# Router by replacement, one-pass biases and a reordered front in a routed-expert transformer block

## The chip, the cores and the metric

The kernel runs on one core of a Trainium2 chip. The metric is the device time of one execution in microseconds, and the median of three runs stands for the kernel. In this text PE is the matrix engine (TensorE), DVE the vector engine, ACT the scalar engine, POOL the GpSimd engine and SP the engine whose queue issues most of the DMAs. An arrow, as in ps<-ring, is output from input.

## The reference

The input is 256 tokens of 1024 numbers, all in float32, one layer. What is computed, cut to the parts that matter here:

```python
h = rmsnorm(x, mix_norm_g);  proj = h @ w_in
gates = sigmoid(proj[..., o_g:] + b_branch_gate)
y_pool = multiscale_pool(u_pool, pool_w, pool_scale) @ pool_up
o = rmsnorm(diff_attention(q, k, v, lam), subln_g) * (1 - lam_init)
y_attn = o @ attn_up
x = x + (g_pool * y_pool + g_attn * y_attn) @ w_out
h2 = rmsnorm(x, ffn_norm_g)
logits = h2 @ router_w + router_b                     # 256 x 32
top_v, top_i = top_k(logits, 4);  top_p = softmax(top_v)
comb = sum(one_hot(top_i, 32) * top_p[..., None], axis=1)
for e in range(32):                                   # three 1024 x 1024 weights each
    g = minimum(h2 @ w_gate[e] + b_gate[e], 7)
    u = clip(h2 @ w_up[e] + b_up[e], -7, 7)
    act = (u + 1) * (g * sigmoid(1.702 * g))
    x = x + comb[:, e] * (act @ w_down[e] + b_down[e])
```

## The kernel before, in words

Every large weight comes in pieces of 2 MB, each 128 rows of 4096 numbers, into a ring of eight slots. SP issues the pieces in the order in which they are used, and before each it waits until the piece that last held the slot has been used. There are 12 pieces of the front (w_in in 8, pool_up, attn_up, and w_out in two column halves, `WO_P` and `WO_P + 1`) and then 192 pieces of the experts, six for each of 32 experts: two of w_gate, two of w_up, two of w_down.

**The front.** Its products are exact enough for float32 by splitting both operands into a high part (ACT, `hi_part`) and a low part (DVE, `lo_part`), each piece in four quarters, and by three one-pass products in the type fp32r (`mm3`). Their results pass through two banks of PSUM in turn ("strips"): the product of strip n has to wait until the reader of strip n-2 has released its bank (`strip_start`, `strip_release`). After the attention, PE computes eight strips of y_pool (`up("pup", ...)`); DVE reads each one, multiplies it with its gate and releases the bank (the loop over `("pup", m)`). Then come four gate strips, the transposes of the attention's heads, four more gate strips, eight strips of y_attn (`up("aup", ...)`) and the four projections `project(t, half)`, token tile t by column half of w_out. DVE adds each projection to the residual stream (`residual`), ACT squares it (`squares2`), PE transposes it (`turn_stream`).

**The router.** PE makes the logits with eight small products in four column groups, ACT copies them out, PE transposes them, DVE adds the four groups. DVE finds the top 8 values (MAX8), their places (FIND_INDEX8), compares them with a row of numbers, and sums the comparisons to `chosen`, a 128 x 32 mask for each token tile. Three products with a triangular matrix and a matrix of ones turn the mask into each token's rank in its expert's list. From the ranks `select` makes the first expert's selection matrix `pick`, PE gathers the expert's tokens (`gather(0)`), ACT copies them, PE transposes them (`turn`), DVE multiplies with the norm's gain into `h_in`, and the loop over the experts begins. Meanwhile DVE counts the rounds (the largest list in blocks of 64 tokens; the engines read the number into a register) and builds the weights `comb_tab`.

**The loop.** For each expert PE runs six `product`s of one piece, 64 tokens wide in column halves that run side by side on two halves of the array, in plain float32. Ahead of each of the three pairs stand the `biases`: two matmuls with a selector `this_e` of the expert's row and `bias_rows`. Between the pairs stand `scatter` of the expert before (after the first pair), and after the second pair `gather` of the next expert and three groups of transposes. DVE, ACT and POOL work beside this.

The loop of SP is the one that ties the experts to the memory:

```python
sp.wait_ge(piece_done, at * (UNROLL * PIECES_PER_EXPERT) + (n - SLOTS + 1))
...
sp.dma_start(ring[:, ORDER[n % SLOTS], :], src).then_inc(slot_in[ORDER[n % SLOTS]], 16)
```

The first eight expert pieces wait for the front's pieces in their slots instead (`LEFT_BY`, `front_piece_free`): the last two of them for the fourth projection, the two before them for the third.

## Time and profile before

| What | Value |
|---|---|
| median of 3 runs | 1121.17 us (1120.26 to 1121.29) |
| profiled execution | 1120.66 us, span 1118.9 us |
| PE busy | 1087.1 us (97%) |
| DVE busy, ACT busy, POOL busy | 280.6, 187.2, 30.3 us |
| DMA | 432.55 MB, queue q1 busy 92.1% of 16 engines' span |
| mean granted clock of PE | 0.993 of full |

The span runs from the first to the last instruction. A granted clock of 1.00 is PE's upper level, 2.4 GHz, and 0.50 the lower, 1.2 GHz. The front lasts to about 194 us, the loop over the experts from there to about 1112 us, and the rest is the last expert's way out.

### The profile page before, as it was taken

Reading aid. Unit: us, or ns where it says so; the run is one execution under the profiler, and the core shown is the slowest. Engines: PE = TensorE matmul, PEld = TensorE weight load, DVE = VectorE, ACT = ScalarE, POOL = GpSimd, SP = SyncE. Lnnn points to the kernel's source line nnn. Section 1 sums busy time; section 2 is a strip of 40 time slices with the busy share of each in tenths; the row PEclk is TensorE's granted clock in tenths of the full one; section 3 lists DMA queues with packets and bytes.
Section 4 is the critical chain, followed back from the end, with each engine's and each line's share of the span. In section 5 each row is a group of like instructions: output and inputs, shape, how many; then the busy total and the mean of one; then the engine's idle time right before and its main releaser. Section 6 shows DMA issues by size and latency. Waiting matters only on the chain.

```text
span 1118.9 us, 13222 instructions
## 1 busy us (share of the span) xinstructions
PE 1087.1 (97%) x5385; PEld 464.6 (42%) x5385; DVE 280.6 (25%) x627; ACT 187.2 (17%) x339; POOL 30.3 (3%) x42
## 2 busy tenths in 40 slices
PE   7998997999999999999999999999999999999998
PEld 3887994333333333333333333333333333333332
DVE  4875655111111111111111111111111111111112
ACT  4656432000010001000100010001000100010000
POOL 0070030000000000000000000000000000000000
PEclk9999998999999999999999999999999999999999
DMA  9724487899999999999999999999999999999995
GB/s 320 275 89 176 151 314 302 342 421 426 428 429 427 428 431 427 428 429 430 426 429 429 429 426 429 430 426 429 429 429 427 429 430 426 429 429 430 427 428 223
DMA packets 43486, 432.55 MB, mean 387 GB/s; under 512 B 5829, under 2 KB 6378, under 8 KB 18890
## 3 DMA queue, kind: packets, MB, share of 16 engines
q1 hardware_dynamic: 42906, 431.60, 92.1%
q10 hardware_dynamic: 560, 0.68, 0.2%
q8 instruction: 13, 0.21, 0.1%
q14 instruction: 7, 0.06, 0.0%
HBM read 431.22 MB, written 1.05 MB: 386 GB/s over the span
## 4 chain that ended last, share of the span: by engine, by line
PE 85%; DVE 10%; ACT 2%; SPq 1%; issue 1%; DMA 1%; DVEq 0%; ACTq 0%
PE ps L751 59%; PE ps L758 8%; PE ps L723 6%; PE ps L716 3%; DVE arena L1327 3%; PE ps L489 2%; PE ps L491 2%; PE ps L490 2%; DVE ring_r L1058 2%; DVE arena L1325 2%; ACT ring_r L812 1%; DMA ring<-in_w_in 1%; SPq L433 1%; PE ps L776 1%; PE ps L710 0%
## 5 line engine op out<-in xcount | busy, mean ns | idle before, releaser
L751 PE MATMUL ps<-ring,arena 128*64 128x512 f32 x3072 | 675.6, 592 | 0.0
L751 PEld LDWEIGHTS ps<-ring,arena 128*64 128x64 f32 x3072 | 221.1, 137 | 438.1 <-issue 438.1
L1315 DVE TENSOR_SCALAR arena<-ps 128x512 f32<-128x512 f32 x32 | 22.1, 692 | 473.2 <-PE ps L751 473.2
L758 PE MATMUL ps<-arena 128*64 128x512 f32 x384 | 102.1, 610 | 1.4 <-issue 0.7
L1325 DVE TENSOR_SCALAR arena<-ps 128x512 f32<-128x512 f32 x32 | 22.1, 692 | 235.5 <-PE ps L751 235.5
L967 ACT COPY arena<-ps 128x512 f32<-128x512 f32 x32 | 18.8, 586 | 325.0 <-PE ps L710 325.0
L723 PE MATMUL ps<-arena 64*128 64x512 f32 x264 | 65.6, 615 | 0.8 <-ACT arena L973 0.8
L710 PE MATMUL ps<-arena 128*64 128x512 f32 x264 | 64.1, 607 | 0.8 <-DVE arena L1260 0.8
L965 ACT ACTIVATE arena<-arena 128x512 f32<-128x512 f32 x32 | 20.1, 629 | 242.8 <-DVE arena L1315 242.8
L973 ACT COPY arena<-ps 128x512 f32<-128x512 f32 x32 | 18.7, 585 | 248.7 <-PE ps L751 248.7
L489 PE MATMUL ps<-ring_r 128*128 128x256 f32 (+1 forms) x192 | 59.7, 311 | 0.6 <-DVE arena_r L1141 0.3
L490 PE MATMUL ps<-ring_r 128*128 128x256 f32 (+1 forms) x192 | 57.7, 301 | 0.0
L491 PE MATMUL ps<-ring_r 128*128 128x256 f32 (+1 forms) x192 | 57.7, 301 | 0.0
L1058 DVE TENSOR_TENSOR ring_r<-ring,ring_r 128x1024 fp32r<-128x1024 f32 x44 | 54.0, 1281 | 7.4 <-ACT ring_r L812 7.2
L716 PE MATMUL ps<-con,arena 128*128 128x128 f32 x260 | 40.8, 280 | 6.2 <-DVE arena L1327 5.4
L812 ACT CAST ring_r<-ring 128x1024 fp32r<-128x1024 f32 x44 | 43.7, 1052 | 18.8 <-PE ps L491 10.8
L716 PEld LDWEIGHTS ps<-con,arena 128*128 128x128 f32 x260 | 28.9, 141 | 36.1 <-DVE arena L1327 33.6
L758 PEld LDWEIGHTS ps<-arena 128*64 128x64 f32 x384 | 21.8, 135 | 51.1 <-issue 42.9
L723 PEld LDWEIGHTS ps<-arena 64*128 64x128 f32 x264 | 22.8, 186 | 43.1 <-issue 43.1
L489 PEld LDWEIGHTS ps<-ring_r 128*128 128x128 f32 x192 | 36.6, 190 | 3.5 <-ACT arena L837 0.6
L490 PEld LDWEIGHTS ps<-ring_r 128*128 128x128 f32 x192 | 36.6, 191 | 1.4 <-issue 0.2
L491 PEld LDWEIGHTS ps<-ring_r 128*128 128x128 f32 x192 | 36.6, 191 | 1.3
(183 smaller groups left out, 590.7 us busy)
## 6 DMA issues: line engine op xcount, KB each, us to landing
ring<-in_exp_w_gate SPq DMA_DIRECT2D x64, 2048.0 KB, 19.6
ring<-in_exp_w_up SPq DMA_DIRECT2D x64, 2048.0 KB, 21.8
ring<-in_exp_w_down SPq DMA_DIRECT2D x64, 2048.0 KB, 21.8
ring<-in_w_in SPq DMA_DIRECT2D x8, 2048.0 KB, 8.7
ring<-in_w_out SPq DMA_DIRECT2D x2, 2048.0 KB, 7.6
xt<-in_x SPq DMA_DIRECT2D x4, 512.0 KB, 6.8
ring<-in_pool_up SPq DMA_DIRECT2D x1, 2048.0 KB, 7.4
ring<-in_attn_up SPq DMA_DIRECT2D x1, 2048.0 KB, 7.3
```

The costliest lines, as they stand in the source:

```text
L489: mm(dst, a[0], b[1], start=start, stop=False)
L490: mm(dst, a[1], b[0], start=False, stop=False)
L491: return mm(dst, a[0], b[0], start=False, stop=stop)
L710: last = mm(ps[BLOCK * half:BLOCK * (half + 1), 6, :], pick[:, buf, t, :], h2[:, t, HALF * half:HALF * (half + 1)], start=(t == 0), stop=( ...
L716: last = tr(ps[:, bank, P * c:P * (c + 1)], src[:, P * c:P * (c + 1)], ident)
L723: last = mm(ps[:, 2 * t + half, :], pickT[rows, P * t:P * (t + 1)], y_e[rows, :], start=False, stop=True, skip_group_check=True)
L751: last = mm(ps[BLOCK * half:BLOCK * (half + 1), bank, :], src[:, c, k % 2, :], slot(n)[:, c, HALF * half:HALF * (half + 1)], start=False, ...
L758: mm(ps[BLOCK * half:BLOCK * (half + 1), bank, :], this_e[:, buf, k, :], bias_rows[:, HALF * half:HALF * (half + 1)], start=True, stop=False)
L812: nc.scalar.copy(quarter(hi, q), quarter(ring[:, n % LAND, :], q)).then_inc(w_hi, 1)
L1058: return v.tensor_tensor(dst, whole_ap, hi.bitcast(F32), ALU.subtract)
L1325: v.tensor_scalar(u1, ps[:, 5, :], LIMIT, -LIMIT, ALU.min, ALU.max).then_inc(expert_step, 1)
L1327: v.scalar_tensor_tensor(out=act_out.rearrange("q (c p) -> q p c", c=4), in0=u1.rearrange("q (p c) -> q p c", c=4), scalar=1.0, in1=gs.rea ...
```

## The change

Six things change together.

1. Beside pool_up's strips, DVE no longer makes three low quarters of the gate piece `GB_P` ahead of the first release. It makes quarter 1 before the sums over the heads, quarter 2 after strip 1 and quarter 3 after strip 2; `head_norms` moves from strip 1 to strip 4. ACT squares the last heads (`head_squares(1)`) ahead of its last two high quarters.
2. The four projections run by halves of w_out: (0,0), (1,0), (0,1), (1,1), with a half's transposes after the next projection. The first half of w_out is thus free after two projections.
3. The logits are made by 16 products with the tokens on the output's partitions (`token_logits`), 8 of them ahead of the last transposes. The copy, the transposes and the sum of four groups go.
4. The chosen experts are found by MATCH_REPLACE: the four largest logits are replaced by a number `NEVER`, and where the result differs from the logits the expert is chosen. The mask, the triangle and the ones are bf16 (`chosen`, `counts`). The softmax is taken over all 32 logits with the mask as factor. The second tile's norm (`normed(1)`) moves behind the mask.
5. A bias is one matmul in fp32r instead of two in float32. `bias_rows` holds the high parts of both column halves and their remainders in four groups of 32 rows, for which SP loads the biases with 12 DMAs of 64 KB ahead of the second half of w_out, ACT copies 128 x 1536, and DVE subtracts 128 x 1536. In the loop `name_expert` is one copy of 128 x 128 instead of three of 128 x 64.
6. POOL gets a fill of `four` and a cast of the triangle and the ones; ACT's three bias DMAs and POOL's fill of the unused bias rows go.

```diff
@@ sync
+                if n == PUP_P + LAND:
+                    for k, name in enumerate(("exp_b_gate", "exp_b_up", "exp_b_down")):
+                        for row in range(4):
+                            half = row // 2
+                            sp.dma_start(bias_raw[E * row:E * (row + 1), k, :],
+                                         A[name][0][:, HALF * half:HALF * (half + 1)]).then_inc(bias_in, 16)
...
@@ tensor
+            def token_logits(t, q):
+                for c in range(4 * q, 4 * q + 4):
+                    last = mm(ps[:, 4 + t, 0:E], x2T[:, c, P * t:P * (t + 1)], rw[:, c, :],
+                              start=(c == 0), stop=(c == NC - 1))
+                return last
...
                         def biases(k, bank):
-                            for half in range(2):
-                                mm(ps[BLOCK * half:BLOCK * (half + 1), bank, :], this_e[:, buf, k, :],
-                                   bias_rows[:, HALF * half:HALF * (half + 1)], start=True, stop=False)
+                            mm(ps[:, bank, :], this_e[:, buf].rearrange("p h s -> p (h s)"), bias_rows[:, k, :],
+                               start=True, stop=False, skip_group_check=True)
...
@@ scalar
+                if step == STEPS_ATT - 1:
+                    head_squares(1)
                 for n, q in ahead[step]:
                     hi_part(n, q)
-            head_squares(1)
...
@@ vector
+            lo_part(GB_P, 1)
             own(head_sums(1))
...
-            for q in range(1, PARTS):
-                lo_part(GB_P, q)
...
-                if m == 1:
+                if m in (1, 2):
+                    lo_part(GB_P, m + 1)
+                if m == 4:
                     head_norms()
...
+            own(v.tensor_copy(four[:, :, 0:TOPK], top[:, :, 0:TOPK]))
+            for t in range(NT):
+                last = v.match_replace(left[:, t, :], four[:, t, :], logit[:, t, :], NEVER)
             own(last)
-            v.tensor_reduce(chosen, eq4.rearrange("p t k e -> p t e k"), AX.X, ALU.add).then_inc(chosen_ready, 1)
...
+            v.tensor_tensor(chosen[:], left, logit, ALU.not_equal).then_inc(chosen_ready, 1)
+            v.tensor_scalar(negtop, top[:, :, 0], -1.0, None, ALU.mult).then_inc(top_ready, 1)
+            normed(1)
```

Where the instructions stand now is seen best row by row. First DVE beside pool_up, from the sums over the second tile's heads to the fourth release. L1058 before (L1078 now) is a low quarter, L1164 (L1182) the release of a pool_up strip, L1113 (L1133) the sums, L1147 (L1168) the next small step. Before:

```order
L1113 TENSOR_REDUCE small<-arena 128x4
L1147 SCALAR_TENSOR_TENSOR small<-small 128x8
L1058 TENSOR_TENSOR ring_r<-ring,ring_r 128x1024 x3
L1164 SCALAR_TENSOR_TENSOR arena<-arena,ps 128x256 x2
L1153 RECIPROCAL small<-small 128x8
```

And of the change:

```order
L1078 TENSOR_TENSOR ring_r<-ring,ring_r 128x1024
L1133 TENSOR_REDUCE small<-arena 128x4
L1168 SCALAR_TENSOR_TENSOR small<-small 128x8
L1182 SCALAR_TENSOR_TENSOR arena<-arena,ps 128x256 x2
L1078 TENSOR_TENSOR ring_r<-ring,ring_r 128x1024
L1182 SCALAR_TENSOR_TENSOR arena<-arena,ps 128x256
```

One low quarter now stands ahead of the sums, none between the sums and the first two releases, and one after the second release.

Second, PE after the last projection, to the first gather. L668 (L687) are transposes of the residual stream, L685 (L693) the logits, L690 the transposes of the logits, L695 (L716) zero fills of PSUM, L698 to L702 (L721 to L725) the ranks and counts. Before:

```order
L668 MATMUL ps<-con,xt 128x128 x8
L685 MATMUL ps<-arena 32x256 x8
L690 MATMUL ps<-con,arena 128x128 x2
L695 MATMUL ps<-zrow 128x512 x4
L698 MATMUL ps<-arena,con 128x32
L699 MATMUL ps<-arena,con 128x32
L700 MATMUL ps<-arena,con 128x32
```

And of the change:

```order
L687 MATMUL ps<-con,xt 128x128 x4
L693 MATMUL ps<-arena 128x32 x8
L687 MATMUL ps<-con,xt 128x128 x4
L693 MATMUL ps<-arena 128x32 x8
L716 MATMUL ps<-zrow 128x512 x4
L721 MATMUL ps<-chosen,counts 128x32
L722 MATMUL ps<-chosen,counts 128x32
```

Half of the logits' products moved ahead of the last transposes, and the transposes of the logits are gone.

Third, DVE from the logits to the ranks. L1204 (L1237) is the norm of a token tile, L1228 (L1256) the finished logits, L1232 (L1260) the top 8, L1251 (L1272) the ranks. Before:

```order
L1204 TENSOR_SCALAR arena<-xt,small 128x128x4 x2
L1226 TENSOR_REDUCE arena<-ps 128x64
L1228 SCALAR_TENSOR_TENSOR arena<-arena,small 128x32 x2
L1232 MAX top<-arena 128x8 x2
L1234 TENSOR_TENSOR topw<-top 128x8
L1237 MAX_INDEX topi<-top,arena 128x8 x2
L1239 CAST topf<-topi 128x16
L1241 TENSOR_TENSOR arena<-con,topf 128x128 x2
L1244 TENSOR_REDUCE arena<-arena 128x64
```

And of the change:

```order
L1256 SCALAR_TENSOR_TENSOR arena<-ps,small,arena 128x32 x2
L1260 MAX top<-arena 128x8 x2
L1263 COPY four<-top 128x2x4
L1265 MATCH_REPLACE arena<-four,arena 128x32 x2
L1267 TENSOR_TENSOR chosen<-arena 128x64
L1268 TENSOR_SCALAR small<-top 128x2
L1237 TENSOR_SCALAR arena<-xt,small 128x128x4 x2
L1272 TENSOR_TENSOR arena<-ps,chosen 128x64
```

The way from the finished logits to the mask has four steps after MAX instead of five wider ones, and the norm of the second tile stands behind the mask and ahead of the ranks.

## Rows read from the trace of the kernel before

**Rows 1.** Busy time by stage, the loop: length; busy of PE, PEld, DVE, ACT, POOL; clock; DMA share; GB/s.

```profile
300.00:1100.00 800.00, 794.82 (x3740) 276.46 (x3740) 134.79 (x334) 82.89 (x146) 0.00 (x0) 1.00 1.01 428
```

**Rows 2.** DMA issues from 300 to 400 us, and from 1060 to 1080 us: KB each, us to landing.

```profile
ring<-in_exp_w_gate SPq DMA_DIRECT2D x8, 2048.0 KB, 13.4
...
ring<-in_exp_w_down SPq DMA_DIRECT2D x2, 2048.0 KB, 32.4
```

**Rows 3.** Timeline of SP's queue: start, length over all issues of the row, operation.

```profile
118.72 12.23 SPq L436 DMA_DIRECT2D ring<-in_w_out  x2
142.96 0.82 SPq L456 DMA_DIRECT2D ring<-in_exp_w_gate  x2
...
198.19 3.76 SPq L456 DMA_DIRECT2D ring<-in_exp_w_up  x2
...
1068.49 3.76 SPq L456 DMA_DIRECT2D ring<-in_exp_w_down  x2
```

**Rows 4.** Timeline of PE over one expert: start, length, operation; L758 biases, L751 products, L710 gather.

```profile
502.34 7.04 PE L751 MATMUL ps<-ring,arena 128*64 128x512 f32 x32
...
510.07 7.04 PE L751 MATMUL ps<-ring,arena 128*64 128x512 f32 x32
...
519.86 7.04 PE L751 MATMUL ps<-ring,arena 128*64 128x512 f32 x32
...
526.73 1.89 PE L710 MATMUL ps<-arena 128*64 128x512 f32 x8
...
531.03 1.46 PE L751 MATMUL ps<-ring,arena 128*64 128x512 f32 x6
```

**Rows 5.** Timeline of PE, first projection: start, length, operation, of one of three products.

```profile
154.07 0.40 PE L489 MATMUL ps<-ring_r,arena_r 128*128 128x512 f32 x1
...
154.77 0.39 PE L489 MATMUL ps<-ring_r,arena_r 128*128 128x512 f32 x1
```

**Rows 6.** The chain that ended last, its end: start, length, work.

```profile
1104.86 6.89 PE ps L751 x32
```

**Rows 7.** Timeline beside pool_up, and ACT's w_out parts: start, length, operation, [idle before].

```profile
99.79 0.47 ACT L862 ACTIVATE arena<-ps,small 128x256 f32<-128x256 f32 x1 [2.06 <-PE ps L491]
...
102.04 0.60 ACT L886 ACTIVATE arena<-ps 128x512 f32<-128x512 f32 x1
...
102.67 0.69 DVE L1113 TENSOR_REDUCE small<-arena 128x4 f32<-128x512 f32 x1 [5.25 <-ACT arena L886]
...
103.48 3.49 DVE L1058 TENSOR_TENSOR ring_r<-ring,ring_r 128x1024 fp32r<-128x1024 f32 x3
...
107.35 0.58 PE L489 MATMUL ps<-arena_r,ring_r 128*128 128x256 f32 x1 [4.33 <-DVE arena L1164]
...
143.34 3.88 ACT L812 CAST ring_r<-ring 128x1024 fp32r<-128x1024 f32 x4
```

**Rows 8.** Busy time by stage, single microseconds, columns as in the first group.

```profile
112.00:113.00 1.00, 1.00 (x6) 1.00 (x6) 0.13 (x1) 0.00 (x0) 0.00 (x0) 0.50 0.00 0
113.00:114.00 1.00, 1.00 (x10) 1.00 (x9) 0.29 (x1) 0.00 (x0) 0.00 (x0) 0.92 0.00 0
...
190.00:191.00 1.00, 1.00 (x4) 0.00 (x0) 0.93 (x4) 0.00 (x0) 0.00 (x0) 0.50 0.99 426
```

**Rows 9.** The chain that ended last, the router: start, length, work.

```profile
177.54 0.70 DVE xt L1194
...
181.04 1.30 DVE arena L1204 x2
182.59 0.43 DVE arena L1228 x2
...
185.92 0.43 PE ps L699 x2
...
187.84 3.70 PE ps L710 x8
...
194.73 6.87 PE ps L751 x32
```

More of the change, by code:

```diff
@@ L27 @@
 I32 = mybir.dt.int32
-U32 = mybir.dt.uint32
 P = 128
@@ L48 @@
 MASKED = -1e30
+NEVER = 3e38
 HALF = 512
@@ L175, in build @@
         pickw = part(2 * NT * 2 * BLOCK).rearrange("p (b t h s) -> p b t h s", b=2, t=NT, h=2)
-        this_e = part(2 * 3 * BLOCK).rearrange("p (b k s) -> p b k s", b=2, k=3)
-        bias_rows = part(D)
+        of_expert = part(2 * E).rearrange("p (h e) -> p h e", h=2)
+        assert taken[0] <= places["p"]
+        taken[0] = places["p"]
+        places["bias"] = taken[0]
+        part(3 * HALF)
+        bias_rows = arena_r[:, places["bias"]:places["bias"] + 3 * HALF].rearrange("p (k n) -> p k n", k=3)
+        places["bias_raw"] = taken[0]
+        bias_raw = arena[:, taken[0]:taken[0] + 3 * HALF].rearrange("p (k n) -> p k n", k=3)
+        places["expert"] = taken[0]
+        part(2 * P)
+        this_e = arena_r[:, places["expert"]:places["expert"] + 2 * P].rearrange("p (b h s) -> p b h s", b=2, h=2)
         rank_tab = part(NT * (ROUNDS + 1) * E).rearrange("p (t n) -> p t n", t=NT)
@@ L350, in build, with wo_count @@
         FRONT = len(front)
+        WO_ORDER = [(0, 0), (1, 0), (0, 1), (1, 1)]
+        def wo_count(t, half):
+            return WO_ORDER.index((t, half)) + 1
         LAND, HIS, H_SLOT = 4, 3, 7
@@ L680, in _ @@
+            pe.wait_ge(zero_row, 1)
             pe.wait_ge(rw_ready, 1)
-            pe.wait_ge(x2T_even, NT)
-            pe.wait_ge(x2T_odd, NT)
-            for k in range(2):
-                for c in range(4):
-                    last = mm(ps[E * c:E * (c + 1), 4, 0:S], rw[:, 4 * k + c, :], x2T[:, 4 * k + c, :],
-                              start=(k == 0), stop=(k == 1))
-            last.then_inc(logit_done, 1)
-            pe.wait_ge(logitT_ready, 1)
-            for t in range(NT):
-                last = tr(ps[:, 6 + t, 0:P], logitT[:, P * t:P * (t + 1)], ident)
@@ L924, in _ @@
                 nc.scalar.copy(m_split[0][:, m, :], gate[:, NC + m, :]).then_inc(m_hi, 1)
+            act.wait_ge(bias_in, 16 * 12)
+            nc.scalar.copy(bias_rows, bias_raw).then_inc(bias_hi, 1)
             def squares2(t, half):
-                act.wait_ge(x2_ready, 2 * t + half + 1)
-                fn(junk2[half], xt[:, t, HALF * half:HALF * (half + 1)], ACT.Square,
+                act.wait_ge(x2_ready, wo_count(t, half))
+                if half:
+                    act.wait_ge(x2_sq, wo_count(t, 0))
+                fn(junk2[t], xt[:, t, HALF * half:HALF * (half + 1)], ACT.Square,
                    accum_out=ss2[:, t, half:half + 1]).then_inc(x2_sq, 1)
@@ L1286, in _ @@
                                    op0=ALU.is_gt, op1=ALU.add).then_inc(rounds_ready, 1)
-            for t in range(NT):
-                last = v.tensor_tensor(eq4w[:, t], eq4[:, t], wide(topw[:, t, :], [P, TOPK, E], 2), ALU.mult)
-            own(last)
-            own(v.tensor_reduce(combf, eq4w.rearrange("p t k e -> p t e k"), AX.X, ALU.add))
+            dve.wait_ge(top_exp, NT)
+            own(v.tensor_tensor(expo, expo, chosen[:], ALU.mult))
+            own(v.tensor_reduce(esum, expo, AX.X, ALU.add))
+            own(v.reciprocal(esum, esum))
+            own(v.tensor_tensor(combf, expo, wide(esum, [P, NT, E], 2), ALU.mult))
             own(v.tensor_copy(comb_tab.rearrange("p t (r e) -> p t r e", e=E),
```

156 lines of the change are left out of this document (76 added, 80 removed).

## The prediction

> **What bounds the kernel now.** I read the busy time by stage first. In the loop PE is busy 794.82 of 800 us, and the DMA engines are full as well, at 428 GB/s [rows 1]. Both can't be the bound, so I asked which gains on the other. The view of the DMA issues answers it: a 2 MB piece lands 13.4 us after its issue early in the loop and 32.4 us after it at the end [rows 2]. A slot is asked for as soon as PE has left it, so a growing time to landing means that PE frees slots faster than the memory fills them. PE needs 531.03 - 502.34 = 28.69 us for an expert [rows 4]. The memory needs, for six pieces of 2.097 MB (12.58 MB) at 428 GB/s, about 29.4 us, 4.9 us a piece. The reader is to see in this that the kernel before is bound by PE, but runs down a reserve of landed pieces by 0.7 us an expert, and that the reserve is nearly used up. The last pair of pieces is issued from 1068.49 on, about 1.9 us apart [rows 3]; with 32.4 us [rows 2] the last piece lands near 1070.4 + 32.4 = 1102.8, call it 1103.1. The last two products run from 1104.86 for 6.89 us [rows 6], so the second starts at 1108.3. The reserve left is 5 us. Whatever PE saves in the loop beyond that is not to be had; the end is then set by when the stream of pieces starts, and the stream's bound start is the end of the first product, 194.73 + 3.44 [rows 9], where SP issues again, at 198.19 [rows 3]. From there to the last landing are 1103.1 - 198.2 = 904.9 us for 184 pieces (184 x 4.9 = 901, the rest first latency and short gaps).
>
> So two numbers matter: how much earlier the first product of the loop ends, and what follows the last landing.
>
> **Part by part: the loop.** A pair of biases is worth the difference of the product pairs' starts less the pair itself: 510.07 - 502.34 = 7.73, less 6.87, is 0.86 us [rows 4]. The new one is a single fp32r product, 512 columns wide. Its nearest row is the projection's: three such products in 154.77 - 154.07 = 0.70 us, 0.233 each [rows 5]. Its bounds are that and 0.43, the step of the float32 products (6.87 us for 16 pairs); I take 0.23, since type and shape agree. PE saves 3 x 0.63 = 1.9 us an expert, and its period falls to 26.8 us, 2.6 under the memory's. Over 32 experts that is 60 us of PE's time. The reserve (the ninth piece, issued when the first product ends, lands some 6 us later and is wanted 26.8 + 9.2 - 3.4 = 32.6 us later) is 26 us and gone after ten experts, and from there PE waits for landings. `name_expert` as one copy lies under PE's products and costs nothing.
>
> In that state the pieces land 4.9 us apart. After the second piece's product PE needs the scatter and a bias, today 519.86 - 516.94 = 2.9, then 2.3 us, so the third piece starts 0.8 us after its landing; the fourth starts at its landing. Then come gather, transposes and a bias, today 531.03 - 526.73 = 4.3 us [rows 4], then 3.7, so the fifth starts 3.44 + 3.7 - 4.9 = 2.2 after its landing and ends 0.8 after the sixth has landed. The end is the last landing + 0.8 + 3.44 (product) + what follows the last product today, 1118.9 - 1111.75 = 7.15 [rows 6]: 11.4 us.
>
> **The front, pool_up.** PE stood idle for 4.33 us until DVE gave the first strip back [rows 7]. The rows say why: DVE waited 5.25 us for ACT's squares at 102.04, which stood behind two high parts, and then made three low quarters, 3.49 us, ahead of the first release. And the granted clock was at 0.50 until 113.1 [rows 8], after that idle time: two strips took 113.08 - 107.35 = 5.7 us where at 1.00 a strip of 12 products of 256 columns takes half as long, 2.8 for both. In the new order the squares come right after the last gate's tanh (99.79 + 0.47 [rows 7]), at about 100.3 to 100.9; the low quarter 1 is done in the wait for them. The sums end at 101.6 (0.69), the small step at 101.8, and the first release at 102.2, before PE is through with the second strip (102.8 = 107.35 - 4.33, less a little). The second release comes at 103.4; a low quarter (1.17 us, a third of 3.49) and a release (0.42) make 1.6 us twice, against 1.4 us a strip on PE, with one strip of slack. So PE doesn't wait, the low quarters are done before the gate strips ask for them, and `head_norms` (about 1.6 us, after strip 4) fits as well. Sum: 4.5 + 2.9 = 7.4 us. What is late next is PE itself: from there to the router it has no wait worth a number, and ACT, DVE and the loads of w_out and of the first expert are released by PE, so all of it shifts. SP's 12 bias loads stand ahead of the second half of w_out. Its queue waits there anyway, 12.23 us for two issues [rows 3]; an issue costs 0.41 (two in 0.82) to 1.9 us (two in 3.76) [rows 3], so 12 cost 5 to 23 us. I take 5, the small end, because the dear ones are issues into a full queue. At the other end w_out's second half is issued 11 us late. Today it is issued at 130.9 and ACT comes to it at 143.34 [rows 7], 12.4 us later; a piece with a free queue needs about 8, so ACT, behind which the copies for the first projection queue, would be late by 6 us. ACT's copy and DVE's subtraction of 128 x 1536 are 1.6 us each by the rate of the low quarters (1.17 for 1024), and they lie under the first projection: without that cover they cost 1.6 us once. POOL's two operations lie under the q and k products.
>
> **The front, router.** I count from P, the end of the last projection, 177.54 [rows 9], to the first product of the loop at 194.73: 17.2 us. Now: 4 transposes 0.45; 8 small float32 products of 128 x 32, 0.215 each, 1.7; 4 transposes 0.45; 8 more, 1.7, with DVE's copy of the last half hidden under the first four. Price: 0.43 for one at clock 0.50 [rows 9], halved for 1.00, since PE is busy throughout. Logits at P + 4.5; today at 182.59, P + 5.05. From there DVE needs 0.43 (logits), 0.3 (MAX), 0.2 (copy), 0.4 (two replacements, bounded by nothing and by the 0.43 of rows of the same shape; taken near it), 0.2 (compare): mask at P + 6.1. Then DVE makes the first scale, 0.2, and the second tile's norm, 1.3 in the row of 181.04, of which the next step waits for 1.1; it now stands ahead of the ranks: P + 7.4. PE's ranks in bf16 are shorter than that in any case. The ranks' way to the gather is today's, 1.0: gather at P + 8.4, today 187.84, P + 10.3. The gather took 3.7 us because the clock was at 0.50 [rows 8, 9]; in the loop it takes 1.9 [rows 4]. From the gather's end to the first product are 194.73 - 191.54 = 3.2 us (copy, transposes, register load, biases), of which 0.85 go with the biases: the first product starts at P + 8.4 + 1.9 + 2.35 = P + 12.65. DVE's other line (rounds, weights, `h_in`) comes out 0.2 us earlier. Sum: 17.2 - 12.65 = 4.5 us with the gather at full clock, 2.7 without.
>
> **The sum.** The first product ends at 198.2 - 7.4 - 4.5 = 186.3. The last landing is 904.9 us later, less 1 us, because PE frees the first pieces' slots closer together and the memory's gaps of the first expert close: 1090.2. Plus 11.4: a span of 1101.6, which is 17.3 us less than 1118.9. The profiled execution took 1120.66 and the median is 1121.17, 0.5 above it: 1103.9 us, rounded to 1104.
>
> **The Trainium skill on the memory's rate.** The row says 428 GB/s at 13 us to landing as well as at 32, so I take it as the limit. The Trainium skill, "DMA: Bandwidth & Descriptors", section "Where 436 GB/s comes from", puts the ceiling of the ports into SBUF at 435 GB/s; by it, as an estimate, 184 pieces take 887 us and the kernel some 1090. The same section has the memory's own limit for one core at about 358 GB/s, with which this trace does not agree.
>
> **The rivals.**
> - The clock falls in the router again (0.27). PE is idle for about 2 us ahead of the gather, with only short work in the 3 us before it; in the kernel before it fell in such a stretch of idle and short work. For the forecast: PE is busier up to there. 1.8 us more: 1105.7.
> - The router gains nothing (0.09): the small products cost more than 0.215, or DVE's order eats it. 1108.4.
> - pool_up's wait moves on (0.07), say to the low parts of the gate piece, and the clock falls there. 1111.3.
> - The memory isn't at its limit at 428 GB/s (0.05), and goes at 435 when more is asked of it. About 1091, PE then still waiting.
> - PE's saving arrives in full (0.02): 32 x 26.8 us from 182.9 on: about 1050. Against it speaks the growth of the time to landing.
> - The slower side (0.05, of which 0.02 within 0.2%): PE now waits up to 1.5 us for each landing, and the clock falls in the loop. A fall costs 2.9 us (pool_up's two strips). PE's period has 2.6 us of room; after the reserve is gone, 23 experts would have to take over 29.9 us each, more than one fall in every expert, to pass 1121. Against it: the 5 us of gaps that PE has in the loop leave the clock at 1.00 over 800 us [rows 1], and the two falls each followed idle time of 2 us or more.
>
> **How the numbers follow.** The forecast has 0.45. Its own range is 1101 to 1106: the bias issues, the small products and the replacements give 2 us up, the gaps of the stream 1 us, the memory's rate 1 us either way. With the first three rivals 0.88 are between 1101 and 1111; I cut at 1100.5 and 1110, which leaves out half of the pool_up case and those beyond. No change for this kernel is within 0.2%, 2.2 us. Even if the front gave nothing, the reserve of 5 us less the 0.8 is gained. Faster 0.95, same 0.02, slower 0.03.
>
> **What the changed profile would show.** No idle PE and clock 1.00 from 100 to 115 us; projections ending near 170; the first loop product near 183; the time to landing rising until some 450 us and then flat near 36 to 39; PE idle about 2.6 us an expert from there, waiting on DMA; last landing near 1090, 11 us ahead of the span's end. Wrong would be: a rate other than 428 GB/s, a clock below 1.00 in the loop, or the first product later than 187.

## The result, and the profile after

The changed kernel takes 1111.0 us (median of four runs, 1110.49 to 1113.43) against 1121.23 us before, a ratio of 0.9914 [0.9896, 0.9931]. It is faster, by 10.2 us where 17 were forecast, and the time lies 1.0 us above the range. The profiled execution took 1111.07 us with a span of 1109.3 us, where the forecast had a span of 1101.6. The working below accounts for these 7.7 us.

PE's and DVE's timeline beside pool_up (start, length, operation, in brackets idle time and who ended it) is what [rows 7] showed before. ACT first, then DVE:

```profile
100.73 0.47 ACT L883 ACTIVATE arena<-ps,small 128x256 f32<-128x256 f32 x1 [2.06 <-PE ps L511]
101.18 0.60 ACT L907 ACTIVATE arena<-ps 128x512 f32<-128x512 f32 x1
101.67 1.99 ACT L833 CAST ring_r<-ring 128x1024 fp32r<-128x1024 f32 x2
...
101.81 0.69 DVE L1133 TENSOR_REDUCE small<-arena 128x4 f32<-128x512 f32 x1 [1.87 <-ACT arena L907]
102.53 0.17 DVE L1168 SCALAR_TENSOR_TENSOR small<-small 128x8 f32<-128x8 f32 x1
102.62 0.42 DVE L1182 SCALAR_TENSOR_TENSOR arena<-arena,ps 128x256 f32<-128x256 f32 x1
104.06 0.42 DVE L1182 SCALAR_TENSOR_TENSOR arena<-arena,ps 128x256 f32<-128x256 f32 x1 [1.02 <-PE ps L511]
104.40 1.22 DVE L1078 TENSOR_TENSOR ring_r<-ring,ring_r 128x1024 fp32r<-128x1024 f32 x1
```

DVE's wait for the squares has shrunk from 5.25 to 1.87 us, and at the second release it is DVE that waits for PE, no longer the other way round. The busy time by stage (columns as in [rows 1]) for pool_up, and then single microseconds of the router:

```profile
99.00:116.00 17.00, 17.00 (x145) 17.00 (x144) 11.36 (x19) 11.44 (x14) 0.00 (x0) 1.00 0.47 161
...
174.00:175.00 1.00, 1.00 (x12) 1.00 (x10) 0.59 (x1) 1.00 (x1) 0.00 (x0) 1.00 0.67 279
175.00:176.00 1.00, 1.00 (x9) 0.92 (x9) 0.17 (x2) 0.13 (x1) 0.00 (x0) 0.95 1.03 442
176.00:177.00 1.00, 1.00 (x5) 0.56 (x5) 0.42 (x3) 0.00 (x0) 0.00 (x0) 0.50 0.95 410
...
188.00:189.00 1.00, 1.00 (x4) 0.24 (x2) 0.00 (x0) 0.00 (x0) 0.00 (x0) 0.50 0.00 0
189.00:190.00 1.00, 1.00 (x6) 0.34 (x4) 0.00 (x0) 0.00 (x0) 0.00 (x0) 0.72 0.00 0
```

pool_up: PE busy without a gap and clock 1.00, as forecast. The router: the granted clock falls to 0.50 at about 175.9, while PE is busy without a gap, and is back only at about 189.6. What PE does in that stretch, from its timeline:

```profile
172.03 1.87 PE L693 MATMUL ps<-arena 128*128 128x32 f32 x16
173.74 0.63 PE L687 MATMUL ps<-con,xt 128*128 128x128 f32 x4
174.21 2.21 PE L693 MATMUL ps<-arena 128*128 128x32 f32 x16
176.36 1.88 PE L716 MATMUL ps<-zrow 1*128 1x512 bf16 x4
...
180.24 3.68 PE L733 MATMUL ps<-arena 128*64 128x512 f32 x8 [1.53 <-DVE arena L1281]
184.70 1.09 PE L739 MATMUL ps<-con,arena 128*128 128x128 f32 x4 [0.78 <-ACT arena L975]
186.06 0.77 PE L779 MATMUL ps<-arena_r 128*128 128x512 f32 x1 [0.27 <-issue]
186.75 6.74 PE L773 MATMUL ps<-ring,arena 128*64 128x512 f32 x24
```

The logits' products (L693), the zero fills (L716), the gather (L733, 3.68 us), the transposes (L739), the bias (L779) and the first half of the first product run in it. SP's queue gives the two marks that the prediction counts with, P (the issue of the next w_gate pair at the end of the last projection) and the end of the first product, against 177.54 and 198.19 before:

```profile
171.79 0.80 SPq L476 DMA_DIRECT2D ring<-in_exp_w_gate  x2
191.82 3.76 SPq L476 DMA_DIRECT2D ring<-in_exp_w_up  x2
```

In the loop, PE's timeline early on, before the reserve is gone (L779 is the bias, L773 the products, L746 the scatter, L733 the gather; [rows 4] is its answer of before):

```profile
401.14 7.09 PE L773 MATMUL ps<-ring,arena 128*64 128x512 f32 x32
408.16 0.51 PE L779 MATMUL ps<-arena_r 128*128 128x512 f32 x1
408.59 7.09 PE L773 MATMUL ps<-ring,arena 128*64 128x512 f32 x32
415.61 1.99 PE L746 MATMUL ps<-arena 64*128 64x512 f32 x8
417.53 0.50 PE L779 MATMUL ps<-arena_r 128*128 128x512 f32 x1
417.96 7.09 PE L773 MATMUL ps<-ring,arena 128*64 128x512 f32 x32
...
428.27 0.50 PE L779 MATMUL ps<-arena_r 128*128 128x512 f32 x1
428.70 2.79 PE L773 MATMUL ps<-ring,arena 128*64 128x512 f32 x12
```

An expert takes 428.70 - 401.14 = 27.56 us, 1.13 less than the 28.69 of before; 1.9 less was forecast. From 578.65 us on PE waits for the memory, first in its timeline and then in the view of its waits (us in total, times, longest):

```profile
808.88 3.65 PE L773 MATMUL ps<-ring,arena 128*64 128x512 f32 x16
813.67 3.65 PE L773 MATMUL ps<-ring,arena 128*64 128x512 f32 x16 [1.14 <-DMA ring<-in_exp_w_gate]
...
PE ps L773 <- DMA ring<-in_exp_w_gate: 20.7, 18, 1.2
PE ps L773 <- DMA ring<-in_exp_w_up: 3.7, 18, 0.2
```

The time to landing of a piece, by the page over all experts 33 to 35 us, and by stretches (20.4 from 300 to 400 us, 25.3 from 400 to 500, 33.7 from 500 to 600, 35.4 from 900 to 1000), rises and then stands still. [Rows 2] had it still rising, with 32.4 at the end. DMA's rate from 600 to 1090 us is 428 GB/s, the same as in [rows 1]. The page's chain has changed its owner: before it was PE to the last, and now

```profile
PE 50%; DMA 39%; DVE 7%; ACT 2%; SPq 1%; issue 1%; DVEq 0%; ACTq 0%
```

and its end, in order of time, with the last expert's second w_up piece as the landing that sets the end:

```profile
1052.32 35.40 DMA ring<-in_exp_w_up
...
1087.77 3.68 PE ps L773 x16
...
1095.14 7.04 PE ps L773 x32
```

The last piece of all, the second of the last w_down pair, has a row of its own in SP's queue, and the view of the DMA issues gives its time to landing. Of the changed kernel, and then of the kernel before:

```profile
1062.10 0.33 SPq L476 DMA_DIRECT2D ring<-in_exp_w_down  x1
ring<-in_exp_w_down SPq DMA_DIRECT2D x1, 2048.0 KB, 35.4
...
1071.92 0.33 SPq L456 DMA_DIRECT2D ring<-in_exp_w_down  x1
ring<-in_exp_w_down SPq DMA_DIRECT2D x1, 2048.0 KB, 33.2
```

So the last landing is at 1062.10 + 35.4 = 1097.5 us now, 905.7 us after the end of the first product, and was at 1071.92 + 33.2 = 1105.1 before, 906.9 us after it.

### The profile page after: what moved, and what is told of

The parts are those of the page before. It is cut to its first block, busy times and chain, and to the rows that moved or that the text cites. A ratio compares the mean times of both kernels' runs of the same rounds, so it can differ in the third digit from the quotient of the medians.

```text
span 1109.3 us, 12547 instructions
## 1 busy us (share of the span) xinstructions
PE 1059.7 (96%) x5106; PEld 450.3 (41%) x5106; DVE 274.5 (25%) x557; ACT 188.6 (17%) x339; POOL 30.0 (3%) x43
## 4 chain that ended last, share of the span: by engine, by line
PE 50%; DMA 39%; DVE 7%; ACT 2%; SPq 1%; issue 1%; DVEq 0%; ACTq 0%
PE ps L773 35%; DMA ring<-in_exp_w_up 19%; DMA ring<-in_exp_w_gate 19%; PE ps L746 3%; PE ps L509 2%; PE ps L510 2%; PE ps L511 2%; PE ps L739 2%; PE ps L779 2%; DVE arena L1346 2%; DVE ring_r L1078 2%; DVE arena L1344 1%; ACT ring_r L833 1%; DMA ring<-in_w_in 1%; SPq L447 1%
## 5 line engine op out<-in xcount | busy, mean ns | idle before, releaser
L773 PE MATMUL ps<-ring,arena 128*64 128x512 f32 x3072 | 689.7, 597 | 24.4 <-DMA ring<-in_exp_w_gate 20.7
L773 PEld LDWEIGHTS ps<-ring,arena 128*64 128x64 f32 x3072 | 211.1, 137 | 442.5 <-issue 384.5
L746 PE MATMUL ps<-arena 64*128 64x512 f32 x264 | 65.6, 615 | 0.8 <-ACT arena L991 0.8
L733 PE MATMUL ps<-arena 128*64 128x512 f32 x264 | 64.0, 607 | 1.5 <-DVE arena L1281 1.5
L1078 DVE TENSOR_TENSOR ring_r<-ring,ring_r 128x1024 fp32r<-128x1024 f32 x44 | 54.2, 1279 | 8.8 <-ACT ring_r L833 8.7
L779 PE MATMUL ps<-arena_r 128*128 128x512 f32 x96 | 48.5, 505 | 0.9 <-issue 0.3
L739 PE MATMUL ps<-con,arena 128*128 128x128 f32 x260 | 41.3, 282 | 6.2 <-DVE arena L1346 5.5
L739 PEld LDWEIGHTS ps<-con,arena 128*128 128x128 f32 x260 | 29.1, 141 | 36.0 <-DVE arena L1346 33.6
L779 PEld LDWEIGHTS ps<-arena_r 128*128 128x128 f32 x96 | 18.0, 187 | 58.3 <-issue 50.0
L746 PEld LDWEIGHTS ps<-arena 64*128 64x128 f32 x264 | 22.8, 186 | 43.1 <-issue 43.1
```

The source lines that it names most:

```text
L733: last = mm(ps[BLOCK * half:BLOCK * (half + 1), 6, :], pick[:, buf, t, :], h2[:, t, HALF * half:HALF * (half + 1)], start=(t == 0), stop=( ...
L739: last = tr(ps[:, bank, P * c:P * (c + 1)], src[:, P * c:P * (c + 1)], ident)
L746: last = mm(ps[:, 2 * t + half, :], pickT[rows, P * t:P * (t + 1)], y_e[rows, :], start=False, stop=True, skip_group_check=True)
L773: last = mm(ps[BLOCK * half:BLOCK * (half + 1), bank, :], src[:, c, k % 2, :], slot(n)[:, c, HALF * half:HALF * (half + 1)], start=False, ...
L779: mm(ps[:, bank, :], this_e[:, buf].rearrange("p h s -> p (h s)"), bias_rows[:, k, :], start=True, stop=False, skip_group_check=True)
L1078: return v.tensor_tensor(dst, whole_ap, hi.bitcast(F32), ALU.subtract)
```

## The experiments

P is taken from SP's queue in each kernel's profile, and so is S, the end of the first product. "Low" is the time for which the clock stood at 0.50 between P and S, summed from the rows of single microseconds.

| Kernel | Median us | Ratio to before | Span | P | S - P | Low | Span - S |
|---|---|---|---|---|---|---|---|
| before | 1121.23 | | 1118.9 | 177.5 | 20.65 | 6.8 | 920.7 |
| changed | 1111.0 | 0.9914 [0.9896, 0.9931] | 1109.3 | 171.8 | 20.03 | 13.7 | 917.5 |
| changed, again | 1109.51 | 0.9904 [0.9889, 0.9919] | 1107.2 | 172.2 | 17.84 | 6.8 | 917.1 |
| pool_alone | 1114.07 | 0.9949 [0.9931, 0.9966] | 1112.5 | 171.2 | 20.64 | 6.8 | 920.7 |
| pool_undone | 1117.02 | 0.9963 [0.9949, 0.9977] | 1115.1 | 178.4 | 19.62 | 10.2 | 917.1 |
| bias_f32 | 1113.3 | 0.9937 [0.992, 0.9954] | 1110.3 | 171.1 | 18.55 | 6.8 | 920.6 |
| no_bias | 1110.48 | 0.9907 [0.9891, 0.9924] | 1108.7 | 171.5 | 21.23 | 13.7 | 915.9 |
| bias_twice | 1110.89 (one run) | | 1109.1 | 171.1 | 19.79 | 10.2 | 918.2 |
| dense_router | 1108.97 | 0.9889 [0.9873, 0.9906] | 1108.5 | 173.2 | 18.36 | 3.4 | 917.0 |
| early_norm | 1108.92 | 0.99 [0.9884, 0.9917] | 1105.6 | 171.1 | 17.49 | 6.8 | 917.0 |
| dense_early | 1108.5 | 0.9885 [0.9868, 0.9901] | 1107.3 | 170.8 | 17.22 | 3.4 | 919.3 |
| spread | 1112.32 | 0.9924 [0.9909, 0.9939] | 1110.8 | 173.4 | 18.62 | 10.2 | 918.8 |
| spread_early | 1110.03 | 0.9909 [0.9894, 0.9924] | 1107.7 | 173.0 | 17.82 | 6.8 | 916.9 |
| spread_dense | 1111.09 | 0.9915 [0.9902, 0.9929] | 1109.3 | 172.6 | 17.87 | 10.2 | 918.8 |

The theory after the result had three parts: the front's gain at pool_up is as forecast; the router's steps are as forecast, and only the clock takes its gain back; and in the loop a single bias costs 0.43 us and more, which does not matter since the memory sets the end. The rivals were that the front's two edits hide each other, that the bound in the loop is still PE, and that the bias' price is one of the type and not of its shape.

**pool_alone: the kernel before with change 1 alone.**

```diff
+                if step == STEPS_ATT - 1:
+                    head_squares(1)
                 for n, q in ahead[step]:
                     hi_part(n, q)
-            head_squares(1)
...
+            lo_part(GB_P, 1)
             own(head_sums(1))
...
-            for q in range(1, PARTS):
-                lo_part(GB_P, q)
...
-                if m == 1:
+                if m in (1, 2):
+                    lo_part(GB_P, m + 1)
+                if m == 4:
                     head_norms()
```

> The kernel before with only the new order beside pool_up. Theory: this part is worth the idle 4.3 us and the half clock after it, 7 us in all, and everything behind it shifts, so the time is 7 us below before, 1114. The loop stays bound by PE with a period of 28.7 us. Rival: the wait moves to another strip or to the gate strips' low parts, and less than 3 us is gained.

It took 1114.07 us. P came at 171.2 instead of 177.5, S - P stayed (20.64 and 20.65), PE waits for no expert's piece, and the span ends 920.7 us after S, as before. So the kernel stays bound by PE from S to the end and carries the gain of pool_up through to it in full.

**pool_undone: the changed kernel without change 1** (the same diff the other way round).

> The changed kernel with the old order beside pool_up. Theory: the stream of expert pieces starts about 7 us later and with it all landings, so 7 us more than the changed kernel, 1118. Rival: in the changed kernel something else sets the start of the loop (the memory, or the router), and less than 3 us are lost.

It took 1117.02 us, with P at 178.4. From it to the changed kernel are 6.0 us in the median, from the kernel before to pool_alone 6.7 (1120.73 beside it): the order beside pool_up and the rest of the change add, and neither hides the other.

**bias_f32: the changed kernel with a bias as two float32 matmuls again.**

```diff
-                            mm(ps[:, bank, :], this_e[:, buf].rearrange("p h s -> p (h s)"), bias_rows[:, k, :],
-                               start=True, stop=False, skip_group_check=True)
+                            for half in range(2):
+                                mm(ps[BLOCK * half:BLOCK * (half + 1), bank, :], this_e[:, buf, half, :].bitcast(F32),
+                                   bias_rows[:, k, :].bitcast(F32), start=True, stop=False, skip_group_check=True)
```

> The changed kernel, but each bias is again two float32 matmuls 64 tokens wide, with the new selector and the new rows read as float32. Theory: PE's period goes back from 27.6 to about 28.7 us, the memory (29.4 us an expert) still catches up only near the end, and the end is PE's: first product's end 191.8 + 913.6 + 7.15 = a span of 1112.5, so 3 us more than the changed kernel. Rival: the one-pass biases are what brought the gain, and 32 x 1.1 = 36 us come back.

It took 1113.3 us; its span ends 920.6 us after S, the figure of the kernels bound by PE, against 917.5. The one-pass bias is worth these 3 us and no more. The medians differ by 2.3 us and the profiles' spans by 1.0, since the clock in the router was low for 6.8 us here and for 13.7 there. PE's timeline there:

```profile
406.85 1.08 PE L780 MATMUL ps<-arena_r 128*64 128x512 f32 x4
407.76 7.04 PE L773 MATMUL ps<-ring,arena 128*64 128x512 f32 x32
414.63 1.03 PE L780 MATMUL ps<-arena_r 128*64 128x512 f32 x4
```

The product pair takes 414.63 - 407.76 = 6.87 us again, where the changed kernel's takes 408.16 - 401.14 = 7.02. The other two pairs of an expert differ less: 6.96 against 7.02 ahead of the scatter, 6.87 against 6.92 ahead of the gather. Together a full-width bias adds 0.26 us to an expert's products.

**no_bias: the changed kernel without the bias matmuls in the loop.** The results lack the experts' biases; the first product of each pair clears its bank instead.

```diff
-                                              start=False, stop=(k % 2 == 1 and c == 3), skip_group_check=True)
+                                              start=(k % 2 == 0 and c == 0), stop=(k % 2 == 1 and c == 3), skip_group_check=True)
...
-                            mm(ps[:, bank, :], this_e[:, buf].rearrange("p h s -> p (h s)"), bias_rows[:, k, :],
-                               start=True, stop=False, skip_group_check=True)
+                            pass
```

> The changed kernel without the bias matmuls in the loop (the biases are left out of the experts' results). Theory: the memory sets the end, so although PE saves another 1.3 to 1.7 us an expert (up to 55 us over 32) the time stays within 1.5 us below the changed kernel's, and PE's waits for landings grow from 24 to some 70 us. Rival: PE's work still counts, and the time falls by 10 us or more.

It took 1110.48 us. From S to the end are 915.9 us instead of 917.5, although PE has some 1.5 us less to do in every expert (3 x 0.43, and 0.26 in the products). Much of that work turned into waiting, in the view of waits:

```profile
PE ps L773 <- DMA ring<-in_exp_w_gate: 45.4, 47, 1.2
```

With the 15.2 us for w_up, PE's waits for pieces are 60.6 us, where the changed kernel's were 24.4 and some 70 were expected. So the changed kernel is bound by the memory, and what PE saves in the loop is not to be had. The Trainium skill, "DMA: Bandwidth & Descriptors", section "Where 436 GB/s comes from", puts the ceiling of the ports into SBUF at 435 GB/s, and the trace's 428 GB/s, unchanged with PE asking earlier, stays under it.

**bias_twice: every bias matmul issued twice.** Both start the sum in their bank anew, so the second writes the same values once more.

```diff
-                            mm(ps[:, bank, :], this_e[:, buf].rearrange("p h s -> p (h s)"), bias_rows[:, k, :],
-                               start=True, stop=False, skip_group_check=True)
+                            for _ in range(2):
+                                mm(ps[:, bank, :], this_e[:, buf].rearrange("p h s -> p (h s)"), bias_rows[:, k, :],
+                                   start=True, stop=False, skip_group_check=True)
```

> The changed kernel with each bias matmul made twice (the second one writes the same once more). It measures what a single full-width fp32r matmul costs between float32 products of half the array's width. Theory: its 0.43 us is 0.21 for the columns and 0.2 for a weight load that nothing hides, and the second one of a pair costs 0.23 or so, so a pair starts the products 0.66 us later. Rival: the type itself runs at half the rate here, and the pair costs 0.86 us.

PE's timeline:

```profile
404.84 0.73 PE L780 MATMUL ps<-arena_r 128*128 128x512 f32 x2
405.51 7.09 PE L773 MATMUL ps<-ring,arena 128*64 128x512 f32 x32
412.52 0.73 PE L780 MATMUL ps<-arena_r 128*128 128x512 f32 x2
```

Two of them take 405.51 - 404.84 = 0.67 us, so one of the two costs 0.24, the projection's price [rows 5], and a single one 0.43. The type doesn't run at half the rate. The product pair behind two of them is not slower than behind one (7.01). The dear step is the one from the full-width bias to the half-width products: the bias behind full-width transposes, in the timeline of the changed kernel above, costs 428.70 - 428.27 = 0.43 as well. The weight loads (PEld) of the kernel before, from a product to a bias, and of the changed kernel, a bias and the product behind it:

```profile
508.35 0.14 PEld L751 LDWEIGHTS ps<-ring,arena 128*64 128x64 f32 x2 [0.29 <-issue]
508.78 0.14 PEld L758 LDWEIGHTS ps<-arena 128*64 128x64 f32 x2 [0.28 <-issue]
...
408.15 0.19 PEld L779 LDWEIGHTS ps<-arena_r 128*128 128x128 f32 x1 [0.81 <-issue]
408.59 0.20 PEld L773 LDWEIGHTS ps<-ring,arena 128*64 128x64 f32 x4 [0.25 <-issue]
```

Before, the loads go on every 0.43 us from product to bias. Now the load of the bias starts at 408.15, when the product pair is through, and not under it, and the next product's load starts at 408.59, when the bias is through. By the Trainium skill, "TensorEngine Tiling (Array Packing)", section "Tiling Modes", a change of the array's tiling drains the engine; the trace agrees: 0.19 us more in the step to the products (0.43 against 0.24), and some 0.10 us in the pair ahead of the bias. In bias_f32 the pair ahead of the scatter, which has another tiling (64 x 128) but the same type, is longer by 0.09 than the one ahead of the gather, so the tiling costs by itself. At the step from the bias to the products type and tiling change together, and no run separates them there.

**dense_router: unread matmuls keep PE dense in the router.** 4, 8 and 14 bf16 matmuls of 128 x 256 into a bank that nobody reads.

```diff
+            pe.wait_ge(counts_ready, 1)
+
+            def dense(n):
+                for _ in range(n):
+                    mm(ps[:, 6, 0:2 * P], counts[:, 0, :], counts[:].rearrange("p k n -> p (k n)"), start=True, stop=True)
+
+            dense(4)
             turn_half(1, 1)
...
-            pe.wait_ge(counts_ready, 1)
+            dense(8)
             pe.wait_ge(chosen_ready, 1)
...
+            dense(14)
             pe.wait_ge(first_pick, 1)
```

> The changed kernel with 26 bf16 matmuls of 128 x 256 that nobody reads on PE in the router: 4 ahead of the last transposes, 8 ahead of the wait for the mask, 14 ahead of the wait for the first selection. Theory: in the changed kernel the clock falls to 0.50 near 176 us, while PE works without a gap, because the small matmuls of 32 columns keep the array little occupied; with full-width work between them it stays at 1.00, the first product ends 3.5 us earlier, and the time falls by as much, to 1107.5. Rival: the fall has another cause (the idle waits after the mask, or the phase of the chip), the clock falls all the same, and the time stays within 1 us of 1111.

**early_norm: the second tile's norm ahead of the wait for the logits.**

```diff
             root_of(1)
+            normed(1)
...
             v.tensor_scalar(negtop, top[:, :, 0], -1.0, None, ALU.mult).then_inc(top_ready, 1)
-            normed(1)
```

> The changed kernel with the second tile's norm ahead of the wait for the logits, where DVE idles 1.4 us, instead of behind the mask. Theory: the ranks and the gather come 1.1 us earlier and the time falls by 1.1, to 1109.9. Rival: DVE's norm then delays the logits by as much, or PE's zero fills at half clock are what the ranks wait for, and nothing is gained.

**dense_early: both, with 4, 8 and 5 unread matmuls.**

> Both: the full-width matmuls (4, 8 and 5) and the early norm. Theory: the gains add up, 4.6 us below the changed kernel, 1106.4, and the first product ends near 187. Rival: the clock falls in spite of them, and only the norm's 1.1 us is left.

dense_router took 1108.97 us, 1.5 more than expected, with a front that started late: ACT took up w_in's second piece at 23.97, against 21.59 to 23.01 in the others. S - P is 18.36, 1.7 us less than in the changed kernel, and the clock was low for 3.4 us only. The unread matmuls have their price: the 14 ahead of the gather outlast the wait that they fill, and the gather starts at P + 10.09 instead of P + 8.45. From the gather to S are 8.27 us, where the changed kernel needs 11.58. early_norm took 1108.92, where 1109.9 was expected: the gather started at P + 7.54 instead of P + 8.45. dense_early took 1108.5, where 1106.4 was expected: its S came at 188.0, 0.6 us ahead of early_norm's, with 0.3 of it from the start, so the two gains hardly add: the unread matmuls put the ranks and the gather back, which starts at P + 9.06 where early_norm's starts at P + 7.54. Its span ends 919.3 us after S and not 917. Its single microseconds, and the gather:

```profile
176.00:177.00 1.00, 1.00 (x5) 0.36 (x4) 0.90 (x8) 0.00 (x0) 0.00 (x0) 0.67 0.95 410
...
179.00:180.00 1.00, 1.00 (x7) 0.49 (x7) 0.96 (x8) 0.00 (x0) 0.00 (x0) 0.63 0.92 393
...
179.83 1.94 PE L740 MATMUL ps<-arena 128*64 128x512 f32 x8
```

The clock falls all the same at 176.3, but it is back at 179.7, and the gather takes 1.94 us, the loop's price [rows 4]; from its start to S are 8.16 us. Of all the runs of dense_router and dense_early, the fastest of each (1107.16 and 1106.52 us) had a mean granted clock of 1.000 over the whole execution, and the others 0.997 or 0.998 (1108.01 to 1110.28 us): they lie 1.4 to 3.1 us below the others. That is one execution of each, and the start of the program alone varies by 2.4 us (below), so it suggests a price of the last fall and does not measure it. dense_early is the fastest of all, but its interval overlaps with that of the changed kernel's second set of runs (0.9889 to 0.9919), so it is only probably the better kernel.

**spread, spread_early, spread_dense: the small products spread out.** Half of the logits' products stand inside the last projection (before its third and sixth group of products), so that fewer stand together; with early_norm's edit, and with 6 unread matmuls before the mask as well.

```diff
-            project(1, 1)
-            turn_half(0, 1)
...
-            token_logits(0, 0)
-            token_logits(1, 0)
...
+            project(1, 1, {2: first_logits, 5: second_logits})
+            turn_half(0, 1)
```

> The changed kernel with the 16 first small logit matmul records (both token tiles, first four chunks) inside the last projection instead of behind it. PE's work is the same, but after the last projection only 8 small products and 8 transposes follow in a row. Theory: the clock falls because of the long row of 32-column matmuls; with half of them between wide ones it falls later than 4.2 us after the last transposes of the first tile begin, or not at all, and the gather and the first products run at 1.00: up to 4 us less than the changed kernel, 1107 to 1109. Rival: the clock falls at the waits behind the mask all the same, the low stretch is as long, and nothing is gained.

> The same with the second tile's norm ahead of the wait for the logits. Theory: another 1.1 us less as long as the norm fits into DVE's wait: 1106 to 1108. Rival: the logits now come 1.7 us earlier after the last projection, so DVE has no wait left for the norm and it delays them instead; then it gains nothing over the kernel above.

> The same with six bf16 matmuls of 128 x 256 that nobody reads ahead of the wait for the mask. Theory: they fill PE's only wait before the ranks, the clock holds at 1.00 up to the gather or is back for it, and the first product ends 16 us after the last projection or earlier: 1106 or less. Rival: the clock falls in spite of them and they only delay the ranks by up to 0.5 us.

All three missed: 1112.32, 1110.03 and 1111.09 us, none of them below the 1109.51 of the changed kernel measured with them. The clock fell in each of them, at 176.9, 179.1 and 178.0, and in two of them once more inside the first product, in spread from 187.1 to 190.5 and in spread_early from 185.9 to 189.3. With half the small products gone from behind the projection, the transposes wait for DVE (0.34 us), and P itself comes 1.8 us later, counted from the start, by the 0.81 us that each group costs inside the projection. In spread and spread_dense the span also ends 918.8 us after S and not 917, which the clock does not explain. So the theory behind them, that the row of 16 small products alone brings the clock down, falls.

**after_again: the changed kernel once more.**

> The changed kernel once more, unchanged, on the chip of the three above, so that they are compared with it there. 1111 us, with the clock at 0.50 from about 4 us behind the last projection; how long it stays there (6 to 14 us in the runs so far) differs from run to run if it is the chip's phase that decides.

It took 1109.51 us, with the same steps as in the first profile up to 176 us. In its single microseconds the clock falls and comes back earlier:

```profile
176.00:177.00 1.00, 1.00 (x7) 0.68 (x7) 0.21 (x2) 0.00 (x0) 0.00 (x0) 0.76 0.99 426
...
183.00:184.00 1.00, 0.83 (x4) 0.00 (x0) 0.59 (x2) 0.12 (x1) 0.00 (x0) 0.82 0.69 295
```

With 6.8 us low instead of 13.7, S - P is 17.84 us instead of 20.03: 2.2 us for 6.8 us of low clock, in the same program. Five profiles have the same work up to the first bias: the two of the changed kernel, bias_f32, bias_twice and no_bias. Their clock was low for 13.7, 6.8, 6.8, 10.2 and 13.7 us, and S - P was 20.03, 17.84, 18.55, 19.79 and 21.23 us, in nearly the same order. The fall itself came 4.1 to 6.8 us behind P, in three of the five with PE busy without a gap up to it and in two (bias_twice, no_bias) behind 1 us of idle time.

## Why the prediction was wrong, step by step

**The bound.** The mechanism is right: PE first waits for a piece at 578.65 us (forecast some 450), the time to landing then stands at 33 to 35 us (36 to 39), the rate stays 428 GB/s and the clock in the loop 1.00. PE waits 24.4 us in 18 experts, 1.4 us in each and not 2.6. The length of the stream was mis-sized, through a reading of the kernel before. The prediction put the second issue of the last pair 1.9 us behind the first, at 1070.4, and so the last landing at 1103.1; the row has it at 1071.92 and the landing at 1105.1. From S to the last landing were thus 906.9 us and not 904.9, and the reserve was 3.2 us and not 5. Less the 1 us that the prediction takes off, that makes 905.9, and 905.7 were measured; forecast were 903.9, which is 1.8 us too few.

**pool_up and the front.** The mechanism is right in each of its parts: no idle PE, clock 1.00, and no wait of PE behind it that was not there before; the 12 bias loads took 5.6 us in SP's queue and no wait of PE comes from them. P was forecast at 170.14 and came at 171.79. Of these 1.65 us, 1.0 is the start of the profile: ACT took up w_in's second piece at 22.62 instead of 21.64. That moment varies from 21.6 to 24.0 between these profiles, and P follows it: 149.2 us later in the changed kernel, in both its profiles, and in early_norm, dense_early and dense_router. That leaves 6.7 us for the term of 7.4, and pool_alone, less its own start, gave 7.2, the 4.33 us of idle time in the row and the 2.9 of the clock; the sum had 4.5 for the 4.33. The rest of the change costs the front some 0.5 us ahead of P, and no run shows by what.

**The router: the step that failed.** Up to the gather everything stands where the working put it: logits at P + 4.75 (P + 4.5), ranks at P + 7.5 (P + 7.4), gather at P + 8.45 (P + 8.4). The prediction halved the price of the small products, "since PE is busy throughout", took "the gather at full clock", and gave 0.27 to a fall that costs the gather's 1.8 us alone. The clock fell while PE was still busy throughout, and it stayed low not for the gather but for 13.7 us: the gather took 3.68 instead of 1.9, from its end to the first product were 2.83 instead of 2.35, and the first product ended 5.07 us after its start instead of 3.44. Together 3.9 us (20.03 against 16.1), more than double what the rival allowed. dense_early, whose clock was back for its gather, sizes the two parts: there the same three steps take 1.94, 2.53 and 3.69 us, so 3.4 of the 3.9 us are the clock's, and 0.5 would be missing at full clock as well. The rival was the right one to name, and a busy PE was the wrong reason against it.

**The loop.** The single bias was sized at 0.23 from a row in which like stands behind like. It costs 0.43, and the products around the three biases take 0.26 us more: 1.13 us saved in an expert instead of 1.9. I had 0.43 as the other bound. The end did not depend on it, as no_bias shows, since the memory took nearly all of it; it moved the point at which the reserve is gone. The 26 us that the prediction gives the reserve, at 29.4 - 27.56 = 1.8 us an expert, last for 14 experts from S, to 578 us.

**The end.** Forecast were 11.4 us from the last landing to the end; there are 1109.3 - 1097.5 = 11.8. The pieces land 4.9 us apart to the last, as forecast. The chain leaves the stream at the third piece from the end, at 1087.77: then the product, the transposes and the bias (7.37 us where the working had 7.14), the last pair (7.04 where it had 6.88) and the way out (7.1).

**The sum.** 1.0 (start) + 0.7 (pool_up) + 3.9 (router, 3.4 of it the clock) + 1.8 (stream) + 0.4 (end) = 7.8 us, the whole difference of the spans but for rounding. With the clock's part as in the second profile of the same kernel, 2.2 us less, the time is inside the range, as the 1109.51 of its second set is. Whether the forecast's range held was thus decided by how long the clock stayed low; 1104 itself would have been missed by some 5 us even so.

**Still open** is what decides how long the clock stays low. It was 3.4 to 13.7 us, 13.7 and 6.8 in the same program; the two kernels with denser work had the shortest (dense_router, dense_early), which one profile of each suggests and does not show. Open as well is why the kernels bound by the memory end 917 us after S in some profiles and 918.8 to 919.3 in others (dense_early, spread, spread_dense), at 428 GB/s in all of them from 300 us on. In these PE waits for pieces in 19 experts and not in 18, so the reserve was gone one expert sooner. No experiment was made on either.

## What to carry to other kernels

A stretch of small matmuls between two dense ones should be costed at both clocks up to the end of the dense work behind it, not only for the one operation that was slow before: here the clock's price was 3.4 us, and a wait-free PE did not prevent it. A matmul's price is taken from a row in which its neighbours have the same shape as its neighbours to be; a full-width one among half-width ones cost 0.43 us instead of 0.23, and up to 0.15 more in the products beside it. The issue of the last piece is read from its own row: halving the length of a row of two put the last landing 2 us too early. When the memory has become the bound, work back from the landing on which the chain hangs, which need not be the last, and stop spending effort on the other engine's loop: some 1.5 us less in each of 32 experts gave 1.6 us in all.

## What the runs showed of the hardware

The granted clock fell to 0.50 at 175.9 us while PE was busy without a gap, with matmuls of 32 columns and transposes in the last 4 us before it. The Trainium skill, "TensorE: Matmul & The Clock Gate", section "What's actually happening", has the clock set by how busy PE has been recently. The profile's busy share does not bear this out here: PE is busy 1.00 in every row from 120 us to the fall, and the clock leaves 1.00 in the row of 175:176. The second piece of w_in was taken up at 21.6 to 24.0 us, by profile, with ACT waiting for its landing, and P moved with it, by up to 2.4 us. The stream of pieces held 428 GB/s from 300 us on, whatever PE did, with a landing every 4.9 us.
